# Last expert layer: the first expert of a token writes x plus its product, the second adds

## What is computed

```python
x = x + mla_mixer(rms_norm(x, mla_norm_w), ...)
h = rms_norm(x, ffn_norm_w)               # x * rstd of the row * gain of the column
x = x + hier_moe(h, ...)                  # the kernel's output

# hier_moe: 64 experts in 8 groups; a token goes to two experts of one group
gate = g_gate[:, None] * e_prob           # one factor for each of its two experts
hid = silu(xblk @ w_gate[e]) * (xblk @ w_up[e])        # 1024 -> 384
yb = hid @ w_down[e]                                   # 384 -> 1024
out = zeros.at[buf_tok].add(yb * buf_gate[:, None])
```

## Time and profile before

| | us |
|---|---|
| median of 3 runs | 2606.43 (2605.69 to 2606.58) |
| the profiled execution | 2605.92 |
| its span, first to last instruction | 2604.2 |
| busy: PE, PEld | 2307.2, 1446.5 |
| busy: DVE, ACT, POOL | 794.9, 637.5, 725.6 |
| DMA traffic | 693.15 MB, mean 266 GB/s |
| chain that ended last, by engine | DMA 22%, PE 5% of the span |

### The profile page before, as it was taken

How to read it: one execution, slowest core, us unless ns; L and a number is a source line. 1 busy time by engine, 2 the same in 40 slices (tenths; PEclk the granted TensorE clock), 3 DMA queues, 4 the chain that set the end, 5 groups by cost and what they waited for, 6 DMA issues and landing times. The chain is left out here.

```text
span 2604.2 us, 36305 instructions
## 1 busy us (share of the span) xinstructions
PE 2307.2 (89%) x12366; PEld 1446.5 (56%) x12366; DVE 794.9 (31%) x2092; ACT 637.5 (24%) x1392; POOL 725.6 (28%) x1084
## 2 busy tenths in 40 slices
PE   7999995988888888869899999999598888888887
PEld 6888783433333333329799989878233333333333
DVE  4222444100000000026688788654400000000001
ACT  5000221111111111124566666642011111111111
POOL 3222111222212122213555555321122222222222
PEclk9999997999999999999999999999799999999999
DMA  5111228999999999993000000113999999999997
GB/s 132 47 48 39 81 82 353 420 423 424 423 423 424 423 424 424 423 381 98 10 10 10 19 10 1 66 49 149 400 414 414 415 413 411 415 416 416 411 416 292
DMA packets 142734, 693.15 MB, mean 266 GB/s; under 512 B 38598, under 2 KB 68294, under 8 KB 97072
## 3 DMA queue, kind: packets, MB, share of 16 engines
q1 hardware_dynamic: 118064, 658.26, 61.6%
q0 software_dynamic: 24576, 33.65, 4.4%
HBM read 679.20 MB, written 46.14 MB: 279 GB/s over the span
## 5 line engine op out<-in xcount | busy, mean ns | idle before, releaser
L1552 PE MATMUL ps<-arena 128*64 128x384 f32 x2048 | 382.2, 531 | 80.4 <-DMA arena<-in_exp_w_up 77.4
L1552 PE MATMUL ps<-gate_up,arena 128*64 128x384 f32 x2048 | 376.0, 523 | 70.3 <-issue 68.6
L1448 DVE TENSOR_TENSOR arena<-ps,xw 128x512 f32<-128x512 f32 x128 | 88.5, 692 | 906.5 <-PE ps L1540 906.3
L1552 PEld LDWEIGHTS ps<-arena 128*64 128x64 f32 x2048 | 155.3, 148 | 275.8 <-issue 230.3
L1552 PEld LDWEIGHTS ps<-gate_up,arena 128*64 128x64 f32 x2048 | 171.2, 146 | 244.2 <-issue 177.2
L996 PE MATMUL ps<-hT_split,w_split 128*128 128x512 f32 x1152 | 264.9, 392 | 8.1 <-DVE hT_split L889 8.1
L1314 ACT ACTIVATE arena<-ps 128x384 f32<-128x384 f32 x128 | 62.9, 491 | 839.1 <-PE ps L1552 839.1
L996 PEld LDWEIGHTS ps<-hT_split,w_split 128*128 128x128 f32 x1152 | 217.0, 189 | 53.7 <-DVE hT_split L889 8.8
L1573 PE MATMUL ps<-arena 128*64 128x512 f32 x960 | 228.6, 612 | 1.1 <-DVE arena L1457 1.1
L1266 POOL DMA_INDIRECT y_rows<-arena,col_idx x64 | 65.4, 1022 | 505.6 <-ACT arena L1326 505.6
L1457 DVE TENSOR_TENSOR arena<-arena,ps 128x192 f32<-128x192 f32 x128 | 45.3, 354 | 414.2 <-ACT arena L1320 414.2
(11 more groups left out here) (261 smaller groups left out, 3416.4 us busy)
## 6 DMA issues: line engine op xcount, KB each, us to landing
arena<-in_exp_w_down SPq DMA_DIRECT2D x80, 1536.0 KB, 28.7
arena<-in_exp_w_gate SPq DMA_DIRECT2D x58, 1536.0 KB, 31.2
arena<-in_exp_w_up SPq DMA_DIRECT2D x58, 1536.0 KB, 35.7
gate_up<-in_exp_w_gate SPq DMA_DIRECT2D x56, 1536.0 KB, 32.1
gate_up<-in_exp_w_up SPq DMA_DIRECT2D x56, 1536.0 KB, 35.9
down<-in_exp_w_down SPq DMA_DIRECT2D x32, 1536.0 KB, 28.6
x<-in_exp_w_down SPq DMA_DIRECT2D x16, 1536.0 KB, 27.6
arena<-in_conv_w_in SPq DMA_DIRECT2D x24, 512.0 KB, 3.7
```

The source lines that it names most:

```text
L1448: dve.tensor_tensor(xT[:, slot, :, :, :].rearrange("p j h m -> p (j h) m"), c.ps[:, slot, :].rearrange("p (a m) -> p a m", m=RANKS), bc(c. ...
L1552: last_ = pe.matmul(c.ps[row:row + RANKS, 2 + slot, 0:FF], xT[:, slot, j, half, :], w_gate_up[w_slot][:, i, (4 * half + j) * FF:(4 * half ...
```

## The change

In the last layer the output rows are no longer begun with `x`. Of the two experts of a token, the one that the kernel comes to first scatters `x` plus its product without adding; the second adds its product in the DMA. So that `x` is at hand, the norm stores natural rows of `x`: each half row is followed by the row factor (516 words, in `x_rows`), and the gathers bring both. The factor rstd comes in with ScalarE's copy of the gate and up products. The `x` stores to `out` and SP's wait for them go. The pieces:

- `act_rows` copies the rows without a factor, then the factor behind both halves; the ring has three tiles, not four.
- `turn_x` takes sixteen products with 64 columns of the identity in place of four transposes, since natural rows are not sorted for the turn.
- Four gather buffers, not two; a gather no longer waits for `x_turned`.
- `find_order` finds the first expert of each token; a fourth part beside the three gate parts takes it to the places (`first_cols`, 16 more products); `split_rows` makes two lists of rows, each out of bounds where the other is not.
- `join_x` on VectorE adds `x` to the first expert's y before the scatter.
- POOL issues a plain scatter, waits for the plain scatter of the expert before, and issues the adding one; `complete` waits for both and now comes behind the next expert's scatters.
- The loops on POOL, ACT and DVE take four experts a turn in place of two, in both layers.

```diff
     def act_rows(self, act, t):
         c = self.c
+        if self.natural:
+            row = self.half_rows(t)
+            act.wait_ge(self.squares, t + 1)
+            act.activation(row[:, :, 0:BANK], c.x[:, t, :].rearrange("p (h d) -> p h d", h=2), ACT.Copy
+                           ).then_inc(self.rows_ready, 1)
+            act.wait_ge(self.rstd_ready, t + 1)
+            act.activation(row[:, :, BANK], bc(c.rstd[:, t], 1, 2), ACT.Copy).then_inc(self.rows_ready, 1)
+            return
...
     def sp_store_rows(self, sp):
         for t in range(NT - 1):
-            self.sp_begin_sums(sp, t)
             self.norm.sp_store(sp, t)
...
         self.experts.load_gate_up(sp, 0, 0)
-        self.sp_begin_sums(sp, NT - 1)
         self.norm.sp_store(sp, NT - 1)
...
+            def scatter_and_add(g, e, slot, n, first_of_round):
+                pool.sem_inc(scatters_begun, 1)
+                for i, idx in enumerate((plain_idx, add_idx)):
+                    pool.tensor_copy(col_idx[:, 2 + 2 * slot + i, :], idx[:, bass.ds(e, 1)]).then_inc(pool_step, 1)
+                pool.wait_ge(pool_step, n + 2)
+                pool.wait_ge(x_joined, g + 1)
+                pool.sem_inc(scatters_begun, 1)
...
+                pool.indirect_dma_start(y_halves, plain, y[:, slot, :], None, bounds_check=2 * S - 1,
+                                        oob_is_err=False).then_inc(scatter_done[slot], 16)
+                if not first_of_round:
+                    pool.wait_ge(scatter_done[1 - slot], (g - 1) * 8 + (16 - 8 * (1 - slot)))
+                    pool.sem_inc(adds_begun, 1)
+                pool.indirect_dma_start(y_halves, add, y[:, slot, :], None, compute_op=ALU.add,
+                                        bounds_check=2 * S - 1, oob_is_err=False).then_inc(add_done[slot], 16)
...
                 if last:
-                    complete(g0 + e - 1, 1 - slot)
-                    scatter(g0 + e, e, slot, n)
+                    scatter_and_add(g0 + e, e, slot, n, False)
                 else:
                     scatter(g0 + e, e, slot, n)
-                    complete(g0 + e - 1, 1 - slot)
+                complete(g0 + e - 1, 1 - slot)
...
-                act.activation(gate_up[:, slot, :], c.ps[:, 2 + slot, 0:FF], ACT.Copy).then_inc(gate_up_copied, 1)
+                scale = gathered[:, e % GATHERED, BANK:BANK + 1] if last else 1.0
+                act.activation(gate_up[:, slot, :], c.ps[:, 2 + slot, 0:FF], ACT.Copy, scale=scale
+                               ).then_inc(gate_up_copied, 1)
...
+            def join_x(g, e, n):
+                slot = n % 2
+                dve.wait_ge(y_copied, g + done(0))
+                dve.scalar_tensor_tensor(out=y[:, slot, :], in0=gathered[:, n % GATHERED, 0:BANK],
+                                         scalar=first_cols[:, bass.ds(e, 1)], in1=y[:, slot, :],
+                                         op0=ALU.mult, op1=ALU.add).then_inc(x_joined, 1)
+
+            def expert(g0, e, n):
+                expert_x(g0 + e + 1, (n + 1) % 2)
+                expert_h(g0 + e, n % 2)
+                if last:
+                    join_x(g0 + e - 1, e - 1, n - 1)
...
-                rows = gathered[:, slot, :].rearrange("p (m j) -> p j m", j=4)
-                for j in range(4):
-                    last_ = pe.transpose(c.ps[:, slot, j * P:(j + 1) * P], rows[:, j, :], c.ident[:, :])
+                if last:
+                    rows = gathered[:, held, 0:BANK].rearrange("p (m j) -> p j m", j=KD)
+                    for k in range(KD):
+                        at = (2 * (k % 4) + k // 4) * RANKS
+                        for row in (0, RANKS):
+                            last_ = pe.matmul(c.ps[row:row + RANKS, slot, at:at + RANKS], rows[:, k, :],
+                                              c.ident[:, row:row + RANKS], start=True, stop=True)
```

226 lines of the change are left out of this document (151 added, 75 removed).

## The result

Over 20 runs of each the changed kernel takes 2610.21 us (2608.36 to 2614.26), the kernel before 2606.57 us (2605.38 to 2608.16). The ratio is 1.0015, with a 95% interval of 1.0009 to 1.0021: 3.6 us slower, where 2.4 us faster was forecast. The profiled execution took 2614.26 us (span 2612.6), 4 us above the median of its kernel and the longest of its 20; a second profile (experiment 18) took 2610.37 with a span of 2608.7 us. Where the two differ, the second is read.

The account below looks back on a forecast made before the run. The prediction took the last layer to be bound by DMA queues full of expert weights, except at its start and end. Terms -8.2 + 2.3 + 0.2 + 3.3 + 0 = -2.4 us gave a median of 2604.0 us, range 2594 to 2616.

Parts of the forecast that it names:

- The accumulating rows: Last layer's scatters: 2048 of 4096 half rows no longer add, at 4.0 ns of all queues' time each: -8.2 us.
- the extra scatter: Last layer's loop: 64 more DMAs without more rows, 0.035 us each by packet time: +2.3 us, 0 to 6.6 kept.
- Wider rows: Last layer's gathers: rows of 2064 B in place of 2048 cost +0.2 us.
- The turn: TensorE's loop: sixteen products take 1.9 us for 0.75; the loop becomes 10.4 us, under the DMAs' 11.97, so hidden.
- the start: Last layer's first experts, TensorE late: two longer turns and 16 more gate products, less 0.4 us back: +3.3 us.
- POOL and VectorE in the loop: Last layer's loop: the longer chain to each gather suffices for loops of 10.8 us, and there are 12: 0.
- rival 2: Last layer's loop: gathers land late behind three DMAs an expert on POOL's queue; +30 us, 2634; chance 0.05.
- The end: Last expert: y(63) comes later, but its adding scatter starts at 2596.3, as before: 0, from -1 to +2.6 us.
- 8 us from the last adding issue to the end, as now: Sign for the forecast at the kernel's end: this time stays unchanged.
- The sum: Whole kernel: all terms give -2.4 us on the profiled execution's 2605.92; with 0.5 to the median, 2604.0.
- Rival 3: Whole kernel: extra DMAs free and a cheap turn, -8.2 us, 2598, or 2594 by packet time; chance 0.23.
- Rival 1: Last layer's loop: TensorE becomes the bound if a turn exceeds 3.5 us; +25 us, 2632; chance 0.10.

Follow-up runs that it names:

- experiment 18: The changed kernel as it is, run and profiled again beside the kernel before: 2610.46 us, ratio 1.0016.
- Experiments 1: The changed kernel with every turn done again by four 128-column transposes instead of sixteen 64-column products, columns in the wrong order: 2605.70 us, ratio 0.9996.
- 9: The changed kernel with the four 128-column transposes in the turns of experts 0 and 1 alone: 2608.92 us, ratio 1.0005.
- 10: The changed kernel with the four 128-column transposes in the turns of experts 0 to 9 alone: 2606.92 us, ratio 1.0000.
- experiment 2: The changed kernel with POOL issuing the gather of expert e+4 ahead of expert e's two scatters instead of behind them: 2610.24 us, ratio 1.0014.
- experiment 4: The changed kernel with the edit of experiment 3, and join(62) put ahead of hidden(63) on VectorE: 2607.75 us, ratio 1.0007.
- experiment 3: The changed kernel with VectorE's one-hot comparisons for a next round moved from the end into the steps of experts 61 and 62: 2608.71 us, ratio 1.0010.

## Why the prediction was wrong, step by step

- **The accumulating rows and the extra scatter** (-8.2 + 2.3): right in kind, and a little better than the -5.9 forecast. Measured 12.08 to 11.95 us an expert, 8.0 us over 64, of which the rows gave 11.4 and the DMA took 3.4. The term said to rest on "the packets themselves" has no base: the 6,929 packets of the earlier trace rows were read as 5,542 rows and 1,387 others, but they are some 87 DMAs of 80 packets, whatever rows these send.
- **Wider rows** (+0.2): nothing to be seen.
- **The turn** (1.9 us, "hidden"): the size was right, 2.04. "Hidden" was right in the steady loop and wrong before it, and this is the step that failed first. The prediction itself said that at the start TensorE is late and nothing hides it, but counted only the two turns ahead of gate_up(1). The weights of the first experts lie ready, and a slot is refilled when TensorE leaves it; so TensorE sets the pace of five loops. The earlier trace rows even named a loop without idle time, and was read as the loop's length only. Forecast for the start +3.3; measured +3.8 at gate_up(1) and +6.9 at gate_up(4). Experiments 1, 9 and 10 show it. That gate_up(1) came near the forecast is luck in part, since two errors cancel: the first turn began 1.6 us later (1852.41 for 1850.80) where up to 0.4 earlier was forecast, and it and gate_up(0) took 1.1 more and 0.5 less, +0.6 where +2.0 was forecast.
- **POOL and VectorE in the loop** (0): right; rival 2 fell in experiment 2.
- **The end** (0): the second step that failed, +4.4 us. The prediction let the plain scatter follow the join at once and the adding one follow it at once. It overlooked that join(62) is queued behind hidden(63), with expert 62's scatters ahead of 63's on POOL, and that POOL's copies of indices meet VectorE's comparisons: 2.0 us more from the copy of y(63) to the last issue, which experiment 4 gives back. And "8 us from the last adding issue to the end, as now" became 10.3; that part is measured and not explained.
- **The sum.** From gate_up(5) on 59 experts gain 0.125 us each, 7.4; the start loses 6.9 and the end 4.4: +3.9, and +3.6 measured. The nearness of the two is luck in part, since the start is read from one trace (counted in weights it is 4.6 to 7.4) and the last turn, for which the prediction had 1.2 us at y(63), stands in no term. Rival 3, a whole saving, had the steady loop nearly right. Rival 1 was right in its mechanism, TensorE as the bound, but placed it in all loops, where it decides in the first five.

## What to carry to other kernels

Before a longer step is called hidden, ask from which loop on: while buffers filled ahead are being used up, the engine that frees them sets the pace, and a loop without idle time in the first rows says so. Work that is moved onto a chain at the end is counted by each engine's order there: what is queued ahead of it, and who shares a port with it. And an indirect DMA is paid by the indices that it is given as well, not by the rows that it sends alone.

## What the runs showed of the hardware

- A scatter of 128 half rows has 80 packets, an adding one 144, however many rows are out of bounds; an adding DMA that sends nothing costs the weight queues 0.09 us in a loop of 11.9.
- Weight rows of a partition in two runs of 6 KB in place of one of 12 KB: 195.8 MB in place of 197.6 in 500 us, 0.9%.
- Two copies of 128 indices on GpSimd take 0.2 us each in the loop, 0.76 and 0.41 at the end of experiment 3, and 1.65 and 2.31 at the same place beside VectorE's comparisons with two inputs in SBUF.
- From the last packet to the end of the span there are 4.5 us in the kernel before, 3.8 with one plain scatter an expert, 7 with a plain and an adding one, also where the last adding one is left out.
